# Masked-sum heads and forget heads of a layer in turn, in place of one kind behind the other

## The reference, cut to what matters

```
for i in range(DEPTH_2):                     # 2 layers
    h = x @ w_in[i]
    o_fox = fox_attention(fq, fk, fv, log_f)         # 6 forget heads:
    #   softmax(q k^T / 8 + c_q - c_k, causal) v,  c = cumsum(log_sigmoid)
    o_sb = stick_breaking_attention(sq, sk, sv)      # 5 masked-sum heads:
    #   z = q k^T / 8;  log_not = log_sigmoid(-z) where strictly earlier
    #   a = exp(log_sigmoid(z) + (sum of log_not behind the key));  a v
    o_dsa = dsa_attention(dq, dk, dv, iq, ik, iw)    # 5 selecting heads:
    #   softmax over the 64 keys with the largest index score
    gates = sigmoid(g)                               # 3 x 1024 channels
    merged = gates0 * (o_fox @ up) + gates1 * (o_sb @ up) + gates2 * (o_dsa @ up)
    x = layer_norm(ALPHA * x + merged @ w_out[i])
    ...                                              # feed-forward part, second norm
```

## Time and profile before

| | |
|---|---|
| time, median of 3 | 1561.5 us (1560.35 to 1569.91) |
| the profiled execution's own time | 1570.09 us |
| its span | 1568.3 us |
| PE busy | 1472.4 us (94%) |
| PE weight loads busy | 1198.7 us (76%) |
| DVE busy | 903.9 us (58%) |
| ACT busy | 695.0 us (44%) |
| mean granted TensorE clock | 0.967 of full speed |

### The profile page before, as it was taken

The page is one execution under the profiler, slowest core; times in us unless marked ns, Lnnn a source line. Parts: engine busy times, 40 slices in busy tenths (PEclk is TensorE's granted clock), DMA queues, the critical chain, the costliest instruction groups (busy, mean ns, idle before and its releaser), DMA issues. The chain is left out here.

```text
span 1568.3 us, 25730 instructions
## 1 busy us (share of the span) xinstructions
PE 1472.4 (94%) x10597; PEld 1198.7 (76%) x10597; DVE 903.9 (58%) x1410; ACT 695.0 (44%) x1168; POOL 58.3 (4%) x73
## 2 busy tenths in 40 slices
PE   5999989988999989999899999998999989999996
PEld 2556767655888879898877888878989887788885
DVE  1653343425656556377586655575657768565655
ACT  3232325433444434376732444453547653344442
POOL 0000530000000000000000000000000000000000
PEclk9999999988999999999999999999999989999998
DMA  9630651006554426433237555524534223846420
GB/s 349 257 108 17 236 185 53 2 1 215 180 192 166 134 82 187 141 108 108 108 108 264 184 195 189 186 82 141 163 109 144 89 89 108 305 177 214 179 89 27
DMA packets 121038, 230.14 MB, mean 147 GB/s; under 512 B 20080, under 2 KB 34672, under 8 KB 120176
## 3 DMA queue, kind: packets, MB, share of 16 engines
q1 hardware_dynamic: 118064, 223.80, 41.0%
q10 hardware_dynamic: 2880, 5.01, 0.9%
HBM read 227.76 MB, written 1.05 MB: 146 GB/s over the span
## 5 line engine op out<-in xcount | busy, mean ns | idle before, releaser
L755 DVE TENSOR_TENSOR work_rounded<-ring,work_rounded 128x1024 fp32r<-128x1024 f32 x208 | 240.9, 1221 | 88.2 <-ACT work_rounded L747 88.1
L716 PE MATMUL psum<-channels_rounded,work_rounded 128*128 128x512 f32 x768 | 278.2, 405 | 0.0
L729 PE MATMUL psum<-work_rounded 128*128 128x512 f32 x1152 | 266.5, 390 | 0.0
L974 PE MATMUL psum<-channels_rounded,ring_rounded 128*128 128x256 f32 x1728 | 251.8, 288 | 2.8 <-PEq L2869 1.6
L747 ACT ACTIVATE work_rounded<-ring 128x1024 fp32r<-128x1024 f32 x208 | 203.2, 1049 | 106.4 <-PE psum L729 102.8
L729 PEld LDWEIGHTS psum<-work_rounded 128*128 128x128 f32 x1152 | 214.6, 188 | 45.5
L974 PEld LDWEIGHTS psum<-channels_rounded,ring_rounded 128*128 128x128 f32 x1728 | 225.6, 193 | 9.7 <-issue 8.8
L718 PE MATMUL psum<-channels_rounded,work_rounded 128*128 128x256 f32 x768 | 218.2, 284 | 0.0
L716 PEld LDWEIGHTS psum<-channels_rounded,work_rounded 128*128 128x128 f32 x768 | 147.3, 192 | 39.1 <-issue 2.5
L718 PEld LDWEIGHTS psum<-channels_rounded,work_rounded 128*128 128x128 f32 x768 | 148.1, 193 | 0.8
L1442 DVE TENSOR_TENSOR ring_rounded<-ring,ring_rounded 128x1024 fp32r<-128x1024 f32 x80 | 94.2, 1198 | 48.4 <-ACT ring_rounded L1246 47.8
(11 more groups left out here) (366 smaller groups left out, 2018.5 us busy)
## 6 DMA issues: line engine op xcount, KB each, us to landing
ring<-in_w_in SPq DMA_DIRECT2D x20, 2048.0 KB, 8.3
ring<-in_w_ff SPq DMA_DIRECT2D x16, 2048.0 KB, 8.4
ring<-in_w_ff_in SPq DMA_DIRECT2D x16, 2048.0 KB, 7.7
ring<-in_w_ff_out SPq DMA_DIRECT2D x16, 2048.0 KB, 7.9
ring<-in_w_mod SPq DMA_DIRECT2D x12, 2048.0 KB, 8.9
ring<-in_w_out SPq DMA_DIRECT2D x6, 2048.0 KB, 7.8
ring<-in_w_in SPq DMA_DIRECT2D x8, 1024.0 KB, 5.7
ring<-in_w_up SPq DMA_DIRECT2D x4, 2048.0 KB, 7.9
```

Source lines behind the costliest of these rows:

```text
L716: pe.matmul(v3(psum[:, 4 + m, :], SEQ), w1[0][:, k, m * P:(m + 1) * P], y_both[:, :, k, :], start=(k == 0), stop=False, skip_group_check=True)
L729: mm = pe.matmul(psum[:, 2 * t + n, :], h[ph][:, kq, t * P:(t + 1) * P], w2[pw][:, kq, n * 512:(n + 1) * 512], start=False, stop=False, sk ...
L755: dve.tensor_tensor(parts.low[i % 2][:, at], ring[:, SLOT * s + 1024 * c:SLOT * s + 1024 * (c + 1)], exact(parts.high[i % 2][:, at]), ALU. ...
L974: mm = pe.matmul(ps[:, at:at + SEQ], u[pw][:, k, col:col + P], y_parts[py][:, k, :], start=((k, n) == (0, 0)), stop=((k, n) == (KC - 1, 2)))
```

## The change

Only the list of heads is another. The forget heads and masked-sum heads alternate, beginning with forget head 0 and ending with forget head 5; the five selecting heads stay last.

```diff
-HEADS = [("fox", h) for h in range(6)] + [("sb", h) for h in range(5)] + [("dsa", h) for h in range(5)]
+HEADS = [("fox", 0)] + [(kind, h + (kind == "fox")) for h in range(5) for kind in ("sb", "fox")]
+HEADS += [("dsa", h) for h in range(5)]
```

## The result

Over eight runs each, the changed kernel takes 1571.04 us (median; 1569.14 to 1576.81) and the kernel before 1563.63 (1557.57 to 1569.91). The ratio is 1.0051, with a 95% interval of 1.0026 to 1.0075: slower by 0.5%, less than the 1% that the prediction called a change. Forecast were 0.45%, and 1568.5 us against a median of then 1561.5. The measured median lies 2.5 us above the forecast one, and the median of before is itself 2.1 us higher over eight runs than over the first three.

A forecast was written before the change was run, and what follows sets the result against it. PE, busy 94%, bounds the kernel, but a longer loop through ACT and DVE paces alternating pairs: 2.2 - 1.0 + 2.3 = +3.5 us a layer, +7.0 in all, giving 1568.5 us from a 1561.5 median; range 1557 to 1575.

The forecast's parts named there:

- PE's need of 13.45 us for a pair: PE's own work for one masked-sum turn (one gate product) plus one forget turn (two): 13.45 us, rotations extra.
- The way through ACT and DVE: From ACT's first instruction of one masked-sum head to the next: 14.52, 16.46, 14.52, 16.91 us, each above PE's 13.45.
- The start and the end of the chain: ACT free for masked-sum head 0 at 668.28; head 4's T after 3.02 us, selecting head 1's S 13.45 later.
- The selecting heads: Last five heads, order kept: ACT catches up during one forget turn, small PE waits go; -1.0 us a layer, bounds 0 and -1.2.
- The clock: Half-speed stretches of PE behind two long waits, 0.6 and 1.7 us: +2.3 us a layer, bounds 0 and 3.4.
- The waits themselves: PE idle 3.0 and 3.5 us in the two pairs with a rotation, ahead of V and T of heads 2 and 4.
- The total: Loops +2.2, selecting heads -1.0, clock +2.3: +3.5 us a layer, +7.0 for both, 0.45%; chance 0.46.
- rival 1: In both layers, the ACT and DVE loop holds but PE's clock does not fall: +1.2 us a layer, 1563.9 us; chance 0.22.
- rival 2: ACT and DVE loop under 13.45 us, PE sets the pace: -5.7 us a layer, 1550.1 us; chance 0.08, half-way case 0.12.
- rival 3: Small matmuls together in every pair, PE's clock falls in each: +11.3 us a layer, 1584 us; chance 0.05.
- ACT loaded no table for a change of kind: Rule against the change: ten more kind changes a layer load ACT tables, some 50 us in both; given chance 0.01.

The follow-up runs named there:

- the top-k rounds are off the way: Changed kernel with the eight top-k rounds in pairs behind S of forget heads 0 to 3, none behind masked-sum heads; ratio to before 0.9957.
- both moves: Changed kernel with top-k rounds in pairs behind S of forget heads 0 to 3 and rotations in turns of forget heads 4 and 5; ratio to before 0.9933.
- the rotations taken out: Changed kernel with the two rotations in the turns of forget heads 4 and 5 instead of masked-sum heads 1 and 3; ratio to before 0.9971.
- all top-k rounds on the way: Changed kernel with the eight top-k rounds in pairs behind S of masked-sum heads 0 to 3, none behind forget heads; ratio to before 1.0161.
- both moves in before's own order: Kernel before, top-k rounds 2, 1, 1, 1, 1, 2 behind forget heads 0 to 5, rotations with forget heads 2 and 4; ratio to before 0.9941.
- the filled kernel: Changed kernel with three unread 384-column matmuls on PE ahead of the wait for transposed probabilities of forget heads 2 and 4; ratio to before 1.0015.
- masked-sum head first: Changed kernel with each pair beginning with its masked-sum head, top-k rounds and rotations not moved; ratio to before 0.9907.
- only masked-sum head 0 in front: Kernel before with only masked-sum head 0 moved to the front of the list of heads; ratio to before 0.9936.

## Why the prediction was right, and where it was off

- **PE's need of 13.45 us for a pair.** Shown where PE binds: 13.49 us between masked-sum heads, in the two pairs without a rotation once the top-k rounds are off the way, and again with both moves. The first rotation, where it lies on PE's path, was put at 0.56 us in the second rival's sum; with both moves that pair takes 14.41 us, so it is 0.9.
- **The way through ACT and DVE.** Its four lengths agree to 0.01 us in three of four pairs of the changed kernel, and in all four once the clock is held. That its parts count as they were added up is shown from both sides: a top-k round taken out shortens it by 1.3 us where PE does not bind, the rotations taken out shorten two pairs to 14.52, and a round put in lengthens it by 1.43.
- **The start and the end of the chain.** From S of forget head 0 to ACT's first instruction of masked-sum head 0 the sum had 668.28 - 655.67 = 12.61 us; it is 12.46. From ACT's first instruction of head 4 to S of selecting head 1 it had 3.02 + 13.45 = 16.47 us; it is 16.62. The two misses of 0.15 us cancel.
- **The selecting heads.** -1.0 was taken, -1.21 is measured, beyond the bound of -1.2 by a hundredth. The waits for L1348 and for L1230 at selecting head 1 are gone, as forecast. The reason given, the forget turn ahead in which ACT catches up, is in part borne out: this part takes 28.45 us in the changed kernel and also with all top-k rounds on the way, where everything ahead of it is latest. But it takes 28.44 us with both moves in before's own order too, where a masked-sum turn stands ahead. So the forget turn is enough but not needed; taking work off the way ahead of this part does the same.
- **The clock** is the term whose parts were mis-sized. Two low stretches of 3.4 us were expected, giving 0.6 + 1.7 = 2.3 us a layer. There is one, of 6.8 us, and it costs 1.98 (the filled kernel's trace) to 2.03 (the third distance). The sums agree by luck: the first was too small and the second is not there. Why the clock fell for so long behind one wait of 2.48 us and not behind one of 1.91 us in the same surroundings is open; with more work on the way it fell behind both.
- **The waits themselves** were to be 3.0 and 3.5 us in V and T together. Counted from T of one masked-sum head to T of the next on PE, less the need of 13.45, the first is 698.43 - 681.99 - 13.45 = 2.99 us, as forecast. The second is 731.90 - 716.06 - 13.45 = 2.39. With the clock held (the filled kernel) it is 727.49 - 710.62 - 13.45 = 3.42: it is shorter in the changed kernel because PE, slowed by the low clock, came late to T of head 3. Of the two, 2.48 and 1.91 us stand ahead of V in the listing.
- **The total.** +3.5 us a layer forecast, +3.04 and +3.19 in the traces, and 0.51% over all runs, 8.0 us, with an interval of 4.1 to 11.7.
- **The rivals.** That the clock does not fall at all (rival 1) is false for the changed kernel and describes the filled one: +1.2 us a layer in the rival, 91.53 + 28.45 - 89.26 - 29.66 = +1.06 in its trace. The way being shorter than PE's need (rival 2) is not the changed kernel's case, but it is the right account of the version with both moves. Low clock in every pair (rival 3) did not come. ACT loaded no table for a change of kind: the trace of the changed kernel has one table load in the second block, as in the earlier trace rows, at 566.4 us and so ahead of the first attention. There are nine more changes of kind in a layer, not ten. The Trainium skill, "ScalarE: Activation LUTs", section "Table sets: the hidden batching unit", puts exponential and logarithm in one set, so that one followed by the other needs no further load; the trace agrees.

## What to carry to other kernels

When every engine walks one list of steps in order, an order of independent jobs is judged by the longest way through the engines that are *not* the bottleneck, from one job of the chained kind to the next, against the bottleneck's work over the same steps. Here alternating the kinds was not good or bad in itself: side work of DVE (top-k rounds, rotations) sat on that way, and moving it to the turns of the other kind turned 0.5% slower into 0.7% faster. The first job of a stage should be one whose inputs are already there: in before's order that alone was worth 0.6%, and more of the saving at the start came from the clock, which no longer falls there, than from the wait itself.

## What the runs showed of the hardware

How long the low clock lasts does not follow from the length of the wait ahead of it:

| PE's wait, us | where | half speed behind it, us |
|---|---|---|
| 1.10 and 1.10 | all top-k rounds on the way, turn of masked-sum head 1, both layers | none |
| 1.21 and 1.23 | kernel before, both layers | 3.4 and 3.4 |
| 1.31 and 1.37 | masked-sum head first, both layers | none |
| 1.69 and 1.69 | only masked-sum head 0 in front, both layers | 6.8 and 3.4 |
| 1.91 and 1.90 | changed kernel, both layers | none |
| 2.48 and 2.49 | changed kernel, both layers | 6.8 and 6.8 |
| 2.79 and 2.77 | all top-k rounds on the way, first layer | 10.2 and at least 9.7 |

The same wait of the same program in the same surroundings can have 6.8 us or 3.4 behind it. The stage's first wait of 2.46 us shows it too, with 6.8 us in most layers and 3.4 in two. PE was busy throughout most of these stretches; the one of 10.2 us began 0.87 us before its wait had ended (9.33 us busy of 10.20). Three matmuls of 384 columns ahead of each wait kept the clock at full speed in both layers and delayed nothing, and the stage got 1.98 us shorter by doing them.
